# Routed experts: the gate and up biases as pairs of 64-row products, and the next block's transposes ahead of the gated product's second half

## The chip, the cores and the metric

The kernel runs on one core of a Trainium2 chip. The metric is the device time of one execution in microseconds (us), as the median of several runs; lower is better.

## The reference, cut to what matters

Two transformer blocks are computed on 512 tokens of width 1024. The change touches only the last part of the second block, the routed experts (a mixture of 32 experts, 4 per token, in blocks of 128 rows):

```python
def expert_block(args):
    xb, e = args                       # 128 gathered rows, one expert
    gt = jnp.minimum(xb @ w_gate[e] + b_gate[e], SWIGLU_LIMIT)
    up = jnp.clip(xb @ w_up[e] + b_up[e], -SWIGLU_LIMIT, SWIGLU_LIMIT)
    hid = gt * jax.nn.sigmoid(SWIGLU_ALPHA * gt) * (up + 1.0)
    return hid @ w_down[e] + b_down[e]
```

Everything is float32 with 1024 columns; the gate and up biases are one row of 1024 each for every expert.

## The kernel before

The program is a row of stages, each with its own instruction streams for TensorE, VectorE, ScalarE, GpSimd and the DMA queue of SyncE, tied together by semaphores that are written out by hand. Nothing reorders the code: each engine runs its stream in the order in which it is written. A float32 product is split by hand into float32r parts: a high part, rounded by ScalarE (a `Copy` into a float32r tile), and a low part, the difference, made by VectorE. Three products (high by high, high by low, low by high) are added in PSUM.

`stage_mix_route` is the stage ahead of the experts. Beside its own work it loads the expert biases (`bias_gate_up`, 32 rows of gate and up) and splits them into `c.bias`: 32 rows hold the high part, the next 32 the low part, the remaining 64 are zero, and gate and up stand side by side in 2048 columns.

`stage_experts` is the stage of the change. It loops over the blocks of 128 rows (`block_of(it, u)`, two to an iteration; u = 0 is called the even block here, u = 1 the odd one; the profile shows 33 blocks). A block has 12 pieces of weights, each 128 by 2048 numbers. Piece p belongs to chunk q = p // 2: chunks 0 and 2 are the two halves of the gate product, 1 and 3 those of the up product, 4 and 5 the down product into `Y`. For each piece SyncE has loaded the raw weights, ScalarE writes `w_hi` (line 3133), VectorE writes `w_lo` (line 3207), each in a ring of four, and TensorE multiplies (lines 3070 to 3072 for gate and up, 3080 to 3082 for down). ScalarE may overwrite a ring place when the piece four earlier is done.

Around these products stand, on TensorE:

- the bias: at the first piece of each of the chunks 0 to 3 one product of `pick` (128 by 128, with a one in the block's expert rows) with 512 columns of `bias` (line 3067); it opens the accumulation;
- `turn_hidden(j, half)` (line 3044): four transposes of one half of the gated product `hid`, after piece 5 for half 0, and in the middle of piece 9 for half 1. It waits for VectorE (`h_ok`), whose last step of that half is line 3232;
- `turn(b, nth)` (line 3037): eight transposes of the next block's gathered rows into `X`, after piece 9, inside a branch that the last block skips. ScalarE and VectorE then split `X` into `x_hi` and `x_lo` (lines 3137, 3138, 3212, 3213), which the next block's first product waits for.

ScalarE takes the transposed half in `hidden(j, half)` (line 3146) ahead of the next block's first `w_hi`, so that piece stands behind the transposes in its queue; VectorE's `hid_lo` (line 3237), its `pick` (line 3218), its next `w_lo` and `x_lo` stand behind it in turn.

Of the kernel before, what the change touches and what calls it, by code (L numbers as in the profile page):

```python
# [8 lines left out]
F32 = mybir.dt.float32  # L9
F32R = mybir.dt.float32r  # L10
# [3 lines left out]
ACT = mybir.ActivationFunctionType  # L14
ALU = mybir.AluOpType
AX = mybir.AxisListType

P = 128
# [2398 lines left out]
def stage_mix_route(nc, c, a):  # L2417
# [5 lines left out]
    with Stage(nc, "route") as s:  # L2423
# [73 lines left out]
        bd_raw = c.xg[0:3 * EXPERTS, 1, :]  # L2497

# [4 lines left out]
        with s.block() as block:  # L2503

            @block.sync
            def _(sp):
# [12 lines left out]
                for h in range(2):  # L2519
                    sp.dma_start(c.y[EXPERTS * h:EXPERTS * h + EXPERTS, :, :], a["bias_gate_up"]).then_inc(bias_in, 16)  # L2520
# [10 lines left out]
            def _(pool):  # L2531
# [7 lines left out]
                pool.wait_ge(y_low, PAIRED)  # L2539
                pool.memset(c.y[2 * EXPERTS:P, :, :], 0.0).then_inc(cleared, 1)  # L2540
                pool.wait_ge(cleared, 1)
                pool.wait_ge(squared, M)
                pool.memset(c.xg, 0.0).then_inc(cleared, 1)
                pool.wait_ge(cleared, 2)
# [86 lines left out]
            def _(act):  # L2631
# [7 lines left out]
                act.wait_ge(bias_in, 32)  # L2639
                act.wait_ge(cleared, 1)  # L2640
                act.activation(c.bias[:].rearrange("e (g n) -> e g n", g=2), c.y, ACT.Copy).then_inc(bias_high, 1)
# [40 lines left out]
            def _(dve):  # L2682
# [17 lines left out]
                lo_rows = c.bias[lows, :].rearrange("e (g n) -> e g n", g=2)  # L2700
                step(dve.tensor_tensor(lo_rows, c.y[lows, :, :], lo_rows.bitcast(F32), ALU.subtract))
# [109 lines left out]
def stage_experts(nc, c, a, out):  # L2811
# [13 lines left out]
    with Stage(nc, "moe") as s:  # L2825
# [5 lines left out]
        pick = s.sb("pick", [P, P], F32R)  # L2831
        slot, xg, y = c.slot, c.xg, c.y
# [79 lines left out]
        with s.block() as block:  # L2912
# [115 lines left out]
            def _(pe):  # L3028
# [19 lines left out]
                def block_of(it, u):  # L3048
                    j = it * 2 + u
                    with pe.If(j < n):  # L3050
                        pe.wait_ge(x_low, j + 1)
                        pe.wait_ge(picked, j + 1)
                        for p in range(PIECES):
# [8 lines left out]
                            if q < 4:  # L3062

                                out = GU[:, q, :]
                                if not second:
                                    o = D * (q % 2) + CHUNK * (q // 2)
                                    pe.matmul(out, pick[:], bias[:, o:o + CHUNK], start=True, stop=False)
# [5 lines left out]
                            else:  # L3073
                                for f in range(2):
                                    if p == 9 and f == 1:
                                        turn_hidden(j, 1)
# [9 lines left out]
                            if p == 9:  # L3086
                                with pe.If(j + 1 < n):
                                    turn(1 - u, it + u)
# [111 lines left out]
            def _(dve):  # L3200
# [14 lines left out]
                def pick_bias(j):  # L3215

                    e = owner_of(dve, j)
                    dve.tensor_tensor(pick[:], c.ident[:, ds(e, 1)].to_broadcast([P, P]),
                                      c.ident[:, ds(e + EXPERTS, 1)].to_broadcast([P, P]), ALU.add).then_inc(picked, 1)
# [20 lines left out]
                dve.sem_inc(w_low, STARTED)  # L3240
# [270 lines left out]
```

## Time and profile before

| | |
|---|---|
| median of 3 runs | 3331.22 us (3329.69 to 3335.95) |
| span of the profiled execution | 3332.1 us |
| mean granted clock of TensorE | 0.973 of full speed |
| TensorE busy with matmuls | 3127.5 us, 94% |
| VectorE busy | 2668.2 us, 80% |
| ScalarE busy | 1817.5 us, 55% |
| experts' block loop | about 2111 us to 3297 us of the span |

The profiled execution's span is the time from its first to its last instruction, and it is 0.9 us above the median of the runs; there is no separate figure for what lies around it. Busy times are shares of the whole span; the stage of the experts is the last third of it. Matmul durations overlap: one lasts 0.39 us from its start to its modelled end, while the next starts 0.23 us after it, so what a matmul costs is read from start to start.

### The profile page before, as it was taken

What the parts mean: (1) busy time and instruction counts of PE and PEld (TensorE: products, weight loads), DVE (VectorE), ACT (ScalarE), POOL (GpSimd) and SP (SyncE); (2) the same over time, 40 slices, a digit from 0 to 9 for tenths busy, and PEclk for the clock granted to TensorE, in tenths of its full rate; (3) what the DMA queues carried; (4) which work ended last, traced back from release to release, by engine and by line L of the source; (5) the groups of instructions that cost most, each with busy time, mean ns of one, the idle gap of its engine ahead of it and who ended that gap; (6) DMA issues with size and microseconds to landing.
All of it is one profiled execution on the core that took longest, in us unless ns stands there. A gap on an engine that the chain in (4) does not pass through costs nothing. (4 is left out here: it accounts for less than half of the span.)

```text
span 3332.1 us, 47952 instructions
## 1 busy us (share of the span) xinstructions
PE 3127.5 (94%) x16376; PEld 2708.8 (81%) x16376; DVE 2668.2 (80%) x3821; ACT 1817.5 (55%) x2211; POOL 834.3 (25%) x516
## 2 busy tenths in 40 slices
PE   7999788999887999999999888799999999999998
PEld 7996677999887888888888766688888888888885
DVE  6895652995496887878888565899999999999997
ACT  4433442334585333333333344578877777877775
POOL 0000102445321444445545100211211211211212
PEclk9999888999998999999999889899999999999999
DMA  5231031335456998999998414699999999999996
GB/s 142 70 83 39 1 127 64 136 119 175 152 228 250 337 343 320 350 341 331 344 358 318 170 29 165 257 364 356 366 368 354 361 371 363 364 373 367 365 371 252
DMA packets 195750, 853.24 MB, mean 256 GB/s; under 512 B 21776, under 2 KB 104336, under 8 KB 151936
## 3 DMA queue, kind: packets, MB, share of 16 engines
q1 hardware_dynamic: 167712, 700.86, 57.4%
q0 software_dynamic: 27936, 151.02, 11.1%
q8 instruction: 64, 1.05, 0.1%
q14 instruction: 38, 0.31, 0.0%
HBM read 810.39 MB, written 59.24 MB: 261 GB/s over the span
## 5 line engine op out<-in xcount | busy, mean ns | idle before, releaser
L3207 DVE TENSOR_TENSOR moe_w_lo<-all_raw,moe_w_hi 128x2048 fp32r<-128x2048 f32 x298 | 676.2, 2287 | 50.6 <-ACT moe_w_hi L3133 48.2
L3133 ACT ACTIVATE moe_w_hi<-all_raw 128x2048 fp32r<-128x2048 f32 x298 | 569.3, 1916 | 80.0 <-PE moe_GU L3072 60.0
L3072 PE MATMUL moe_GU<-moe_w_hi,moe_x_lo 128*128 128x512 f32 x1056 | 412.3, 390 | 0.0
L3071 PE MATMUL moe_GU<-moe_w_lo,moe_x_hi 128*128 128x512 f32 x1056 | 412.2, 390 | 0.0
L3070 PE MATMUL moe_GU<-moe_w_hi,moe_x_hi 128*128 128x512 f32 x1056 | 411.7, 390 | 0.0
L1889 DVE SCALAR_TENSOR_TENSOR experts_pair<-experts_pair,all_x_first 128x1024 f32<-128x1024 f32 x128 | 156.4, 1222 | 142.6 <-DMA experts_pair<-in_peer_pairs,experts_slot 142.6
L1733 POOL DMA_INDIRECT experts_pair<-in_peer_pairs,experts_slot x128 | 222.4, 1738 | 114.7 <-POOL experts_slot L1730 110.0
L1264 POOL TENSOR_TENSOR score_w_lo<-all_hT,score_w_hi 128x1024 fp32r<-128x1024 f32 x67 | 165.2, 2467 | 303.7 <-DVE all_x_lo L1380 161.4
L1730 POOL COPY experts_slot<-all_pair_id 128x1 uint32 x128 | 152.8, 1194 | 334.1 <-DVE all_h L1901 304.4
L2976 POOL DMA_INDIRECT pair_rows<-all_mixT,all_slot x32 | 48.8, 1526 | 738.2 <-ACT all_mixT L3175 738.2
L3071 PEld LDWEIGHTS moe_GU<-moe_w_lo,moe_x_hi 128*128 128x128 f32 x1056 | 198.6, 188 | 42.1
L3072 PEld LDWEIGHTS moe_GU<-moe_w_hi,moe_x_lo 128*128 128x128 f32 x1056 | 198.6, 188 | 41.7
L3070 PEld LDWEIGHTS moe_GU<-moe_w_hi,moe_x_hi 128*128 128x128 f32 x1056 | 199.0, 188 | 40.6
L3207 DVE TENSOR_TENSOR moe_w_lo<-all_hT,moe_w_hi 128x2048 fp32r<-128x2048 f32 x98 | 222.5, 2284 | 0.1
L3080 PE MATMUL moe_Y<-moe_w_hi,moe_hid_hi 128*128 128x512 f32 x528 | 212.3, 402 | 0.8 <-DVE moe_hid_lo L3237 0.8
L3082 PE MATMUL moe_Y<-moe_w_hi,moe_hid_lo 128*128 128x512 f32 x528 | 206.2, 391 | 0.0
L3081 PE MATMUL moe_Y<-moe_w_lo,moe_hid_hi 128*128 128x512 f32 x528 | 205.8, 390 | 0.0
L3133 ACT ACTIVATE moe_w_hi<-all_hT 128x2048 fp32r<-128x2048 f32 x98 | 187.7, 1915 | 32.5 <-PE moe_GU L3072 18.7
L1749 PE MATMUL experts_H<-all_x_hi,experts_wd_hi 128*128 128x384 f32 x512 | 173.6, 339 | 20.0 <-DVE experts_wd_lo L1871 19.9
L1288 PE MATMUL score_H<-all_x_hi,score_w_hi 128*128 128x384 f32 (+1 forms) x544 | 190.3, 350 | 1.4 <-DVE all_x_lo L1380 1.4
L1290 PE MATMUL score_H<-all_x_hi,score_w_lo 128*128 128x384 f32 (+1 forms) x544 | 189.6, 349 | 0.0
L1289 PE MATMUL score_H<-all_x_lo,score_w_hi 128*128 128x384 f32 (+1 forms) x544 | 189.6, 349 | 0.0
(546 smaller groups left out, 8108.7 us busy)
## 6 DMA issues: line engine op xcount, KB each, us to landing
all_raw<-in_w_moe SPq DMA_DIRECT2D x149, 2048.0 KB, 9.8
all_hT<-in_w_moe SPq DMA_DIRECT2D x49, 2048.0 KB, 9.7
all_hT<-in_peer_wdT SPq DMA_DIRECT2D x128, 512.0 KB, 8.8
all_wu<-in_peer_pairs SPq DMA_DIRECT2D x64, 1024.0 KB, 10.5
peer_gates<-gates_out SPq DMA_DIRECT2D x6, 4096.0 KB, 11.6
experts_gt<-peer_gates SPq DMA_DIRECT2D x32, 768.0 KB, 9.7
all_hT<-in_w_in SPq DMA_DIRECT2D x40, 512.0 KB, 3.8
all_hid<-peer_early SPq DMA_DIRECT2D x60, 192.0 KB, 7.6
```

Of the source, the lines that this page charges most:

```text
L1288: pe.matmul(out, left, c.x_hi[:, k, at:T], start=(k == 0), stop=False)
L1289: pe.matmul(out, left, c.x_lo[:, k, at:T], start=False, stop=False)
L1290: mm = pe.matmul(out, low, c.x_hi[:, k, at:T], start=False, stop=(k == KD - 1))
L1733: pool.indirect_dma_start(out=pair[:, v, :], out_offset=None, in_=a["peer_pairs"][:, :], in_offset=bass.IndirectOffsetOnAxis(ap=slot[:, n: ...
L3070: pe.matmul(out, x_hi[:, kx, :], hi[:, k, :], start=False, stop=False)
L3071: pe.matmul(out, x_hi[:, kx, :], lo[:, k, :], start=False, stop=False)
L3072: mm = pe.matmul(out, x_lo[:, kx, :], hi[:, k, :], start=False, stop=(kx == KD - 1))
L3080: pe.matmul(Y[:, b, :], hid_hi[:, h, :], hi[:, f, cols], start=(h == 0), stop=False)
L3081: pe.matmul(Y[:, b, :], hid_hi[:, h, :], lo[:, f, cols], start=False, stop=False)
L3082: mm = pe.matmul(Y[:, b, :], hid_lo[:, h, :], hi[:, f, cols], start=False, stop=(h == KD - 1))
L3133: act.activation(w_hi[p % RING][:], piece_of(r, p), ACT.Copy).then_inc(w_high, 1)
L3207: dve.tensor_tensor(w_lo[p % RING][:], piece_of(r, p), w_hi[p % RING][:].bitcast(F32), ALU.subtract).then_inc(w_low, 1)
```

## The change

In `stage_experts`, the four bias products of 128 rows by 512 columns per block become four of 64 rows by 512 columns. They are issued as two pairs: at piece 0 the first halves of gate (rows 0 to 63) and up (rows 64 to 127), at piece 4 the second halves. The two of a pair write different PSUM banks. So `bias` now holds gate high, gate low, up high, up low in four groups of 32 rows and 1024 columns, and `pick` has ones in four rows; it is a copy of a column of a new tile `sel`, which VectorE builds with three additions at the start of the stage. Also, the eight transposes of the next block (with their branch) stand in the middle of piece 9, ahead of the wait and the four transposes of the gated product's second half, where they stood after piece 9.

In `stage_mix_route` the biases are loaded by four DMAs instead of two, ScalarE's split is 1024 columns wide instead of 2048, VectorE's low part is two operations of 32 by 1024 instead of one of 32 by 2048, and GpSimd's clearing of rows 64 to 127 is gone.

```diff
@@ stage_mix_route
-                for h in range(2):
-                    sp.dma_start(c.y[EXPERTS * h:EXPERTS * h + EXPERTS, :, :], a["bias_gate_up"]).then_inc(bias_in, 16)
+                for i in range(4):
+                    sp.dma_start(bias_raw[EXPERTS * i:EXPERTS * i + EXPERTS, :], a["bias_gate_up"][:, i // 2, :]).then_inc(bias_in, 16)
...
-                pool.wait_ge(y_low, PAIRED)
-                pool.memset(c.y[2 * EXPERTS:P, :, :], 0.0).then_inc(cleared, 1)
-                pool.wait_ge(cleared, 1)
...
-                act.wait_ge(bias_in, 32)
-                act.wait_ge(cleared, 1)
-                act.activation(c.bias[:].rearrange("e (g n) -> e g n", g=2), c.y, ACT.Copy).then_inc(bias_high, 1)
+                act.wait_ge(bias_in, 64)
+                act.activation(c.bias[:], bias_raw, ACT.Copy).then_inc(bias_high, 1)
...
@@ stage_experts, TensorE
-                                if not second:
-                                    o = D * (q % 2) + CHUNK * (q // 2)
-                                    pe.matmul(out, pick[:], bias[:, o:o + CHUNK], start=True, stop=False)
+                                if not second and q % 2 == 0:
+                                    half = slice(CHUNK * (q // 2), CHUNK * (q // 2) + CHUNK)
+                                    for g in range(2):
+                                        own = slice(2 * EXPERTS * g, 2 * EXPERTS * g + 2 * EXPERTS)
+                                        pe.matmul(GU[:, q + g, :], pick[own, :], bias[own, half], start=True, stop=False)
...
                                     if p == 9 and f == 1:
+                                        with pe.If(j + 1 < n):
+                                            turn(1 - u, it + u)
                                         turn_hidden(j, 1)
...
-                            if p == 9:
-                                with pe.If(j + 1 < n):
-                                    turn(1 - u, it + u)
@@ stage_experts, VectorE
-                    dve.tensor_tensor(pick[:], c.ident[:, ds(e, 1)].to_broadcast([P, P]),
-                                      c.ident[:, ds(e + EXPERTS, 1)].to_broadcast([P, P]), ALU.add).then_inc(picked, 1)
+                    dve.tensor_copy(pick[:], sel[:, ds(e, 1)].to_broadcast([P, P])).then_inc(picked, 1)
...
+                step = chained(dve, chain)
+                step(dve.tensor_tensor(sel[:], c.ident[:, 0:EXPERTS], c.ident[:, EXPERTS:2 * EXPERTS], ALU.add))
+                step(dve.tensor_tensor(sel[:], sel[:], c.ident[:, 2 * EXPERTS:3 * EXPERTS], ALU.add))
+                step(dve.tensor_tensor(sel[:], sel[:], c.ident[:, 3 * EXPERTS:4 * EXPERTS], ALU.add))
                 pick_bias(0)
```

The first place is TensorE at the start of a block. Before, one bias product opens the gate's accumulation (and another stands 25 rows further down, ahead of the up product):

```order
L3061 ISA [waits route_slot_ok,route_ge_high]
L3067 MATMUL moe_GU<-all_bias,moe_pick 128x512 [waits moe_w_low]
L3070 MATMUL moe_GU<-moe_w_hi,moe_x_hi 128x512
L3071 MATMUL moe_GU<-moe_w_lo,moe_x_hi 128x512
L3072 MATMUL moe_GU<-moe_w_hi,moe_x_lo 128x512
```

Now both stand there, and none ahead of the up product (line numbers shift by one):

```order
L3060 ISA [waits route_slot_ok,route_ge_high]
L3068 MATMUL moe_GU<-all_bias,moe_pick 128x512 [waits moe_w_low]
L3068 MATMUL moe_GU<-all_bias,moe_pick 128x512
L3071 MATMUL moe_GU<-moe_w_hi,moe_x_hi 128x512
L3072 MATMUL moe_GU<-moe_w_lo,moe_x_hi 128x512
L3073 MATMUL moe_GU<-moe_w_hi,moe_x_lo 128x512
```

The up bias has moved ahead of 24 products of the gate, and the same holds at piece 4. (The names in brackets are semaphores by number; those of other stages are reused ones.)

The second place is TensorE in piece 9. Before, the gated product's transposes stand between the two halves of the piece, and the next block's after it:

```order
L3082 MATMUL moe_Y<-moe_w_hi,moe_hid_lo 128x512
L3042 REGISTER_ALU
L3044 MATMUL moe_GU<-all_ident,moe_hid 128x128 [waits moe_h_ok]
L3044 MATMUL moe_GU<-all_ident,moe_hid 128x128 x3
L3080 MATMUL moe_Y<-moe_w_hi,moe_hid_hi 128x512
L3081 MATMUL moe_Y<-moe_w_lo,moe_hid_hi 128x512
L3082 MATMUL moe_Y<-moe_w_hi,moe_hid_lo 128x512
...
L3087 COMPARE_AND_BRANCH
L3034 ISA
L3037 MATMUL moe_X<-all_ident,all_mixT 128x128 [waits norm_meaned]
L3037 MATMUL moe_X<-all_ident,all_mixT 128x128 x7
L3087 UNCONDITIONAL_BRANCH
```

Now they come first, with their branch:

```order
L3085 MATMUL moe_Y<-moe_w_hi,moe_hid_lo 128x512
L3077 COMPARE_AND_BRANCH
L3033 ISA
L3036 MATMUL moe_X<-all_ident,all_mixT 128x128 [waits norm_meaned]
L3036 MATMUL moe_X<-all_ident,all_mixT 128x128 x7
L3077 UNCONDITIONAL_BRANCH
L3041 REGISTER_ALU
L3043 MATMUL moe_GU<-all_ident,moe_hid 128x128 [waits moe_h_ok]
L3043 MATMUL moe_GU<-all_ident,moe_hid 128x128 x3
L3083 MATMUL moe_Y<-moe_w_hi,moe_hid_hi 128x512
```

The wait on `h_ok` now stands behind the eight transposes and the end of their branch, and the four transposes of the gated product behind both.

## Rows read from the trace of the kernel before

**Rows 1.** Busy time by engine, 180 us of the experts' loop; a count behind each.
```profile
core 0: us, PE busy (x) PEld busy (x) DVE busy (x) ACT busy (x) POOL busy (x), PEclk, DMA share, GB/s
2300.00:2480.00 180.00, 179.33 (x825) 147.53 (x824) 171.22 (x125) 141.73 (x106) 34.92 (x21) 1.00 0.94 362
```

**Rows 2.** Bias products of before, all: min/median/max ns, first and last start.
```profile
L3067 PE MATMUL moe_GU<-all_bias,moe_pick x132: 389/389/787, 2111.1 to 3278.8; 128*128 128x512 f32 x132
```

**Rows 3.** Timeline of PE, a bias product and the 24 behind it: start, duration.
```profile
2554.82 0.39 PE L3067 MATMUL moe_GU<-all_bias,moe_pick 128*128 128x512 f32 x1
2555.05 0.39 PE L3070 MATMUL moe_GU<-moe_w_hi,moe_x_hi 128*128 128x512 f32 x1
...
2560.26 0.39 PE L3072 MATMUL moe_GU<-moe_w_hi,moe_x_lo 128*128 128x512 f32 x1
```

**Rows 4.** Timeline of PE, attention: 64-row products between others, in five short windows.
```profile
1987.37 0.27 PE L2265 MATMUL attn_X<-all_ident,attn_sc 128*128 128x128 f32 x1
1987.57 0.49 PE L2252 MATMUL attn_S<-all_kT,all_qT 64*128 64x256 f32 x2
1987.89 0.39 PE L2252 MATMUL attn_S<-all_kT,all_qT 64*128 64x256 f32 x2
1988.10 0.39 PE L2252 MATMUL attn_S<-all_kT,all_qT 64*128 64x256 f32 x2
1988.32 0.39 PE L2252 MATMUL attn_S<-all_kT,all_qT 64*128 64x256 f32 x2
1988.64 0.34 PE L2277 MATMUL attn_O<-attn_pT,all_vtok 128*64 128x128 f32 x2
```

**Rows 5.** Timeline of PE in the last block: a product after a wait.
```profile
3292.22 0.49 PE L3080 MATMUL moe_Y<-moe_w_hi,moe_hid_hi 128*128 128x512 f32 x1 [0.83 <-DVE moe_hid_lo L3237]
3292.54 0.39 PE L3081 MATMUL moe_Y<-moe_w_lo,moe_hid_hi 128*128 128x512 f32 x1
```

**Rows 6.** Timeline of PE, piece 9 of an even block.
```profile
2570.50 0.39 PE L3082 MATMUL moe_Y<-moe_w_hi,moe_hid_lo 128*128 128x512 f32 x1
2571.22 0.66 PE L3044 MATMUL moe_GU<-all_ident,moe_hid 128*128 128x128 f32 x4 [0.33 <-DVE moe_hid L3232]
...
2571.96 0.40 PE L3081 MATMUL moe_Y<-moe_w_lo,moe_hid_hi 128*128 128x512 f32 x1
...
2572.89 0.39 PE L3082 MATMUL moe_Y<-moe_w_hi,moe_hid_lo 128*128 128x512 f32 x1
2573.12 1.03 PE L3037 MATMUL moe_X<-all_ident,all_mixT 128*128 128x128 f32 x8
2574.11 0.49 PE L3080 MATMUL moe_Y<-moe_w_hi,moe_hid_hi 128*128 128x512 f32 x1
2574.44 0.39 PE L3081 MATMUL moe_Y<-moe_w_lo,moe_hid_hi 128*128 128x512 f32 x1
```

**Rows 7.** Timeline of PE, piece 9 of the odd block after it.
```profile
2606.70 0.40 PE L3082 MATMUL moe_Y<-moe_w_hi,moe_hid_lo 128*128 128x512 f32 x1
2606.93 0.60 PE L3044 MATMUL moe_GU<-all_ident,moe_hid 128*128 128x128 f32 x4
...
2607.61 0.39 PE L3081 MATMUL moe_Y<-moe_w_lo,moe_hid_hi 128*128 128x512 f32 x1
...
2608.52 0.39 PE L3082 MATMUL moe_Y<-moe_w_hi,moe_hid_lo 128*128 128x512 f32 x1
...
2610.05 0.39 PE L3081 MATMUL moe_Y<-moe_w_lo,moe_hid_hi 128*128 128x512 f32 x1
```

**Rows 8.** Waits from 2120 us on: us in total, times, longest.
```profile
PE moe_GU L3044 <- DVE moe_hid L3232: 5.5, 16, 0.5
```

**Rows 9.** Timelines of ACT, DVE and PE, end of that odd block, next block's start.
```profile
2607.57 0.60 ACT L3146 ACTIVATE moe_hid_hi<-moe_GU 128x512 fp32r<-128x512 f32 x1 [2.43 <-PE moe_GU L3044]
2612.82 0.68 DVE L3213 TENSOR_TENSOR moe_x_lo<-moe_X,moe_x_hi 128x512 fp32r<-128x512 f32 x1
2615.30 0.39 PE L3067 MATMUL moe_GU<-all_bias,moe_pick 128*128 128x512 f32 x1
```

**Rows 10.** Timeline of DVE and ACT, route stage and start of the experts.
```profile
2044.11 1.92 ACT L2641 ACTIVATE all_bias<-all_mixT 128x2048 fp32r<-128x2048 f32 x1 [8.75 <-DMA all_mixT<-in_bias_gate_up]
2094.81 0.23 DVE L2788 TENSOR_SCALAR route_ecmp<-route_end,route_part 128x32 f32<-128x32 f32 x1
2107.30 2.33 DVE L3207 TENSOR_TENSOR moe_w_lo<-all_raw,moe_w_hi 128x2048 fp32r<-128x2048 f32 x1 [0.74 <-ACT moe_w_hi L3133]
```

More of the change, by code:

```diff
@@ L2497, in stage_mix_route @@
         bd_raw = c.xg[0:3 * EXPERTS, 1, :]
+        bias_raw = c.y[:, 0, :]
         ranks, total = acc[:, 0, 0, 0:M * EXPERTS], acc[:, 0, 0, M * EXPERTS:(M + 1) * EXPERTS]
@@ L2538, in _ @@
                 pool.wait_ge(made, 4)
-                pool.wait_ge(y_low, PAIRED)
-                pool.memset(c.y[2 * EXPERTS:P, :, :], 0.0).then_inc(cleared, 1)
-                pool.wait_ge(cleared, 1)
                 pool.wait_ge(squared, M)
                 pool.memset(c.xg, 0.0).then_inc(cleared, 1)
-                pool.wait_ge(cleared, 2)
+                pool.wait_ge(cleared, 1)
                 pool.wait_ge(saved, 16 * M)
@@ L2699, in _ @@
                 lows = slice(EXPERTS, 2 * EXPERTS)
-                lo_rows = c.bias[lows, :].rearrange("e (g n) -> e g n", g=2)
-                step(dve.tensor_tensor(lo_rows, c.y[lows, :, :], lo_rows.bitcast(F32), ALU.subtract))
+                up_lows = slice(3 * EXPERTS, 4 * EXPERTS)
+                dve.tensor_tensor(c.bias[lows, :], bias_raw[lows, :], c.bias[lows, :].bitcast(F32), ALU.subtract)
+                step(dve.tensor_tensor(c.bias[up_lows, :], bias_raw[up_lows, :], c.bias[up_lows, :].bitcast(F32), ALU.subtract))
                 dve.wait_ge(bd_high, 1)
@@ L2831, in stage_experts @@
         pick = s.sb("pick", [P, P], F32R)
+        sel = s.sb("sel", [P, EXPERTS])
         slot, xg, y = c.slot, c.xg, c.y
@@ L3273, in _ @@
                     block_of(it, 0)
-                step = chained(dve, chain)
                 def first_row(m):
@@ L3423, in routed @@
         self.xg, self.y = pairs[:, 0, :, :], pairs[:, 1, :, :]
-        self.bias = self.sb(ctx, "bias", [P, 2 * D], F32R)
+        self.bias = self.sb(ctx, "bias", [P, D], F32R)
         self.geT = self.sb(ctx, "geT", [3 * EXPERTS, M, P], F32R)
```

## The prediction

> **What bounds the kernel now.** I read the page first, then the loop of the experts in 180 us windows, then TensorE's timeline product by product, then the waits of that stretch, and last what the other engines do at a block's end. In the loop TensorE is busy 179.33 of 180 us at full clock (1.00), VectorE 171.22, ScalarE 141.73 [rows 1]. A busy TensorE proves little, since its records overlap, so the pitch counts: from the first to the last of the 24 products behind a bias product it is 5.21 us over 23 steps, 0.2265 us each, and the bias product takes the same step (2554.82 to 2555.05) [rows 3]. Nothing stands between them. So in this loop a product removed from TensorE is 0.2265 us off the end, and one added is as much on it, as long as VectorE keeps up; over this window VectorE has 5% left.
>
> Only two kinds of place leave TensorE's pitch: the transposes, and one wait. The wait is for the gated product (VectorE's line 3232). From 2120 us on, 16 waits of more than noise are put down to it, 5.5 us of PE's idle time [rows 8]. They are one in every second block: the even block shows 0.72 us from the last product to the first transpose [rows 6], the odd one 0.23 [rows 7]. The last of the 16 is in the last block, so 15 lie in blocks that have a next one.
>
> **Part 1, the pairs.** There are 132 bias products [rows 2], four to a block, so 33 blocks and 66 places where a pair will stand. If nothing but the products counted, a pair that runs at once would replace two steps (0.453 us) by one. What it takes to go from 128-row products to 64-row ones and back isn't shown in this loop, but attention shows it at full speed [rows 4]:
> - into the 64-row form: transposes there follow each other at 0.109 us (as the eight of the next block do: 1.03 us less the last one's 0.27, over 7 steps [rows 6]), but the first 64-row products start 0.20 us after the last: 0.09 lost;
> - the weights of the first two can't be loaded ahead: first two to second two 0.32 us, where later ones follow at 0.215 (1987.89 to 1988.32 in two steps): 0.10 lost;
> - out of it: 0.32 us from the last two to the next form, instead of 0.215: 0.10 lost;
> - the first product after it has its own weights exposed: a product that starts cold is followed after 0.32 us instead of 0.2265 [rows 5]: 0.10 lost.
>
> That is 0.39 us of switching to save one step of 0.2265: +0.165 us a place, 66 x 0.165 = **+10.9 us**. The lower bound is a pair that takes one step and nothing else: 66 x 0.2265 = -14.9 us. The upper bound is a pair that doesn't run at once: 66 x 0.39 = +25.7 us. I take the middle value because it is the only one that rows of this case show on both sides of a 64-row stretch.
>
> The Trainium skill (TensorEngine Tiling (Array Packing), Key Properties) says that changing the tiling mode drains TensorE; by that rule, the rows of attention agree, with their 0.09 and 0.10 us. The skill's other page on this (TensorE: Matmul & The Clock Gate, Part 3, Measured speedup vs the span model) gives a pack as one matmul plus some 4 ns for each further tile, with no term for entering or leaving; by it the pairs would save about 14.7 us, and that is my first rival below.
>
> **Part 2, the transposes moved.** I count from the last product before a group of transposes to the second product after it, less two steps. Even block: 2570.50 to 2571.96, less 0.453, is 1.01 us for the four of the gated product with their wait; 2572.89 to 2574.44 is 1.55, less 0.453, 1.10 us for the eight; together 2.11 [rows 6]. Odd block: 0.91 and 1.53 us, less 0.453 each: 0.46 and 1.08, together 1.54 [rows 7]. Afterwards they stand in one run: 0.23 from the product to the first of eight, 7 x 0.109 = 0.76 to the last, then the end of the branch. That end costs something today: the last of the eight starts at 2573.88, the next product at 2574.11, 0.23 later, and is followed after 0.33 [rows 6]. I take 0.23 for it again, then 0.39 for the starts of four transposes with a cold first one (0.66 less 0.27), and 0.35 to the second product: 1.96 less 0.453 = 1.51. So an even block gains 0.60, an odd one 0.03: 15 x 0.60 + 17 x 0.03 = **-9.5 us**. If the branch's end hides under transposes, 0.12 and the 0.06 of the cold start go as well, at most 32 x 0.18 = 5.8 us more. The wait itself must then be over: in the even block the gated product is there at 2571.2, and TensorE would now come to it at 2570.50 + 0.23 + 0.76 + 0.23 = 2571.7, even without the pairs' delay. It has 0.5 us to spare.
>
> **What comes late by it.** The gated product's transposes in an odd block start about 0.76 + 0.23 + 0.33 (the two pairs of that block) = 1.3 us later than now. Behind them in ScalarE's queue are line 3146, the next block's first high part and both halves of `x_hi`; in VectorE's queue `hid_lo`, `pick`, the next low part and `x_lo`. The last of these ends now at 2613.50, the next block starts at 2615.30 [rows 9]: 1.8 us of cover. TensorE itself moves by 0.3, so 0.8 us of cover is left. In an even block the delay is smaller, since the transposes there wait already. ScalarE has 2.43 us idle ahead of line 3146 [rows 9], which takes the delay first. I cost it at nothing; once the cover is gone it costs one for one.
>
> The up bias now comes ahead of the gate's 24 products, which ends the first piece pair 0.39 us later and the second 0.165 later. VectorE's first use of the gate comes far later than the piece's end, and the banks were read before `h_ok` of the block before.
>
> **The rest.** `sel` is three small operations; one of 32 columns takes 0.23 us and VectorE's next step there waits 0.74 us for ScalarE [rows 10], so about 0.1 us shows, once. `pick` as a copy is no longer than before and isn't waited for. In the route stage ScalarE waited 8.75 us for the biases' DMA and then took 1.92 for the split [rows 10]; half as wide it takes about 0.9 less, and four DMAs move the same bytes. Bounds are 1 us either way, and I take 0, since TensorE's products cover that stretch.
>
> **Sum.** +10.9 - 9.5 + 0 = +1.4 us on the profiled execution of 3332.1 us, 3333.5; its span is 0.9 us above the median of the runs, so against that median 3331.2 + 1.4 = **3332.6 us**. No change that can be told: about 0.2% (6.7 us) is what a measurement of this kernel can tell from none.
>
> **Rivals.**
> - *Switching is cheap for float32r* (faster). Attention's products are float32, each two records, and what starts together there may differ from a pair on two row halves. Without any switching cost: -14.9 - 9.5 = -24.4, 3306.8 us; with half of the 0.39 us paid: 66 x (0.195 - 0.2265) = -2.1, with the moves -11.6, 3319.6. For it: these products are twice as long, so loads may hide. Against it: in attention neither load nor drain was hidden. It decides for faster once a place costs under +0.04 us. 25%.
> - *The two of a pair run one after the other* (slower). The two records that start together in attention could be the two of one float32 product. Then a place costs +0.39: +25.7 - 9.5 = +16.2, 3347.4 us. It decides for slower once a place costs over (6.7 + 9.5) / 66 = 0.245 us. 13%.
> - *The wait moves instead of going* (slower). The later transposes use up the 0.8 us of cover and the next block's first product waits for `x_lo`, or VectorE, at 95%, falls behind. If it eats the whole gain: +10.9, 3342 us; 8%.
> - *The change does what its parts cost here* (no change), 54%, with its own range of 3327 to 3338 us.
>
> **How the numbers follow.** The forecast's 54% is almost all of "same"; I put same 0.53, faster 0.26, slower 0.21. The range of 3310 to 3346 us leaves out the pair without any switching (about 11%) and most of the pair in series.
>
> **What the changed profile would show.** (1) The two bias products of a pair start some 10 to 20 ns apart, in the 64-row form. If 0.23 us or more apart, the second rival holds. (2) Last 128-row product to the pair 0.32 us, pair to first product 0.42, that to the second 0.32: in all about 1.07 us from the last product to the second one after the pair, where 0.91 was spent before, one of its four steps further down. If near 0.70, the first rival. (3) PE's waits for line 3232 gone but in the last block, and in both kinds of block 1.96 us from the product before the transposes to the second one after. (4) No wait of TensorE for `x_lo` at a block's start. (5) Block pairs still 71.8 us long or within 0.2 of it. What would make me wrong is (2), since it counts 66 times, and the end of the branch, which counts 32 times.

## The result: 30 us slower, and what the profile after shows

| | before | after |
|---|---|---|
| median of 4 runs beside each other | 3333.59 us (3329.69 to 3336.48) | 3363.59 us (3356.14 to 3367.86) |
| ratio | | 1.0092 (1.0076 to 1.0109) |
| span of the profiled execution | 3332.1 us | 3366.1 us |

The forecast was 3332.6 us, "no change that can be told", with a range of 3310 to 3346. The kernel is slower by 0.9%, outside the range. The page of the changed kernel, first the span, then busy time by engine:

```profile
span 3366.1 us, 47955 instructions
...
PE 3162.9 (94%) x16376; PEld 2694.2 (80%) x16376; DVE 2674.8 (79%) x3825; ACT 1818.3 (54%) x2211; POOL 831.0 (25%) x515
```

The same 180 us of the experts' loop as in [rows 1], columns as there:

```profile
2300.00:2480.00 180.00, 179.57 (x802) 141.31 (x803) 168.01 (x123) 135.91 (x103) 36.30 (x20) 1.00 0.92 352
```

TensorE is as full as before, at the same granted clock (1.00), and gets through 802 matmul records where it got through 825. VectorE and ScalarE do less in the same time, so they aren't the bound: TensorE's own stream has become slower. The page's share of busy time doesn't show it; only the count and the pitch do.

The length of a block is read from TensorE's timeline: the first bias product of the 3rd and of the 33rd block, 30 blocks apart. Before:

```profile
2184.48 0.39 PE L3067 MATMUL moe_GU<-all_bias,moe_pick 128*128 128x512 f32 x1
...
3261.48 0.39 PE L3067 MATMUL moe_GU<-all_bias,moe_pick 128*128 128x512 f32 x1
```

And after:

```profile
2188.88 0.51 PE L3068 MATMUL moe_GU<-all_bias,moe_pick 64*128 64x512 f32 x2
...
3295.20 0.50 PE L3068 MATMUL moe_GU<-all_bias,moe_pick 64*128 64x512 f32 x2
```

(3261.48 - 2184.48) / 30 = 35.90 us a block, and (3295.20 - 2188.88) / 30 = 36.88: 0.98 us more. Over 33 blocks that is 32 us, about the whole loss, so other stages have no part in it that can be told. Two blocks together take 73.8 us, where the prediction had 71.8 within 0.2. This block length repeats better than a single execution's span, because the loop's first bias product starts anywhere between 2104 and 2114 us in the executions profiled here. I use it below beside the medians.

Three places of a block answer to the steps of the prediction. First the pair, TensorE's timeline at a block's start:

```profile
2483.49 0.40 PE L3085 MATMUL moe_Y<-moe_w_hi,moe_hid_lo 128*128 128x512 f32 x1
2483.82 0.51 PE L3068 MATMUL moe_GU<-all_bias,moe_pick 64*128 64x512 f32 x2
2484.25 0.50 PE L3071 MATMUL moe_GU<-moe_w_hi,moe_x_hi 128*128 128x512 f32 x1
2484.59 0.40 PE L3072 MATMUL moe_GU<-moe_w_lo,moe_x_hi 128*128 128x512 f32 x1
```

The two of the pair stand in one row (x2); their single records start 3 to 4 ns apart, where 10 to 20 was forecast. From the last product to the second one behind the pair it is 1.10 us, and 1.07 was forecast.

Second, products with nothing between them, the first and the last of 15 in a row:

```profile
2498.23 0.40 PE L3071 MATMUL moe_GU<-moe_w_hi,moe_x_hi 128*128 128x512 f32 x1
...
2501.49 0.39 PE L3073 MATMUL moe_GU<-moe_w_hi,moe_x_lo 128*128 128x512 f32 x1
```

14 steps in 3.26 us: 0.2324 us each (from the unrounded starts; 0.233 from the rows). In [rows 3] it is 0.2265. The prediction took this pitch as given. Nothing in the diff touches these products.

Third, the moved transposes in piece 9 and the start of piece 10:

```profile
2511.69 0.40 PE L3085 MATMUL moe_Y<-moe_w_hi,moe_hid_lo 128*128 128x512 f32 x1
2511.93 1.04 PE L3036 MATMUL moe_X<-all_ident,all_mixT 128*128 128x128 f32 x8
2512.80 0.60 PE L3043 MATMUL moe_GU<-all_ident,moe_hid 128*128 128x128 f32 x4
2513.15 0.48 PE L3083 MATMUL moe_Y<-moe_w_hi,moe_hid_hi 128*128 128x512 f32 x1
2513.47 0.39 PE L3084 MATMUL moe_Y<-moe_w_lo,moe_hid_hi 128*128 128x512 f32 x1
...
2514.41 0.40 PE L3085 MATMUL moe_Y<-moe_w_hi,moe_hid_lo 128*128 128x512 f32 x1
2514.89 0.49 PE L3083 MATMUL moe_Y<-moe_w_hi,moe_hid_hi 128*128 128x512 f32 x1
```

The transposes are as cheap as hoped, and cheaper: 1.78 us from the product before them to the second behind them, with 1.96 forecast. The four start 0.11 us behind the last of the eight (2511.93 + 7 x 0.109 = 2512.69), so the end of the branch costs nothing. But six products later stands a gap that I hadn't forecast: 0.48 us from 2514.41 to 2514.89, where a step is 0.23. The waits of TensorE from 2120 us on name it, beside the two of the pairs (us in total, times, longest):

```profile
PEld moe_GU L3068 <- issue: 23.9, 65, 0.4
...
PEld moe_Y L3083 <- issue: 16.8, 32, 0.5
...
PEld moe_GU L3071 <- issue: 16.1, 65, 0.2
```

32 times line 3083: once in each block that has a next one, ahead of piece 10. The wait for the gated product of [rows 8] is gone.

### The profile page after: what moved, and what is told of

Same layout as the page of the kernel before. It is cut to its first block and busy times, and to the rows that moved or that the text cites. A ratio compares the mean times of both kernels' runs of the same rounds, so it can differ in the third digit from the quotient of the medians.

```text
span 3366.1 us, 47955 instructions
## 1 busy us (share of the span) xinstructions
PE 3162.9 (94%) x16376; PEld 2694.2 (80%) x16376; DVE 2674.8 (79%) x3825; ACT 1818.3 (54%) x2211; POOL 831.0 (25%) x515
## 5 line engine op out<-in xcount | busy, mean ns | idle before, releaser
L3071 PE MATMUL moe_GU<-moe_w_hi,moe_x_hi 128*128 128x512 f32 x1056 | 427.2, 405 | 0.0
L2975 POOL DMA_INDIRECT pair_rows<-all_mixT,all_slot x32 | 68.2, 2131 | 754.6 <-ACT all_mixT L3175 754.6
L1730 POOL COPY experts_slot<-all_pair_id 128x1 uint32 x128 | 144.2, 1127 | 342.3 <-DVE all_h L1901 312.7
```

What stands on the lines that cost most here:

```text
L3071: pe.matmul(out, x_hi[:, kx, :], hi[:, k, :], start=False, stop=False)
```

## Theories

The loss has three candidates: **addresses** (the slower pitch comes from where the tiles now lie: `bias` is 4096 bytes a partition smaller, and `sel`, 128 bytes a partition, stands behind `pick` and in front of `x_hi`), **pairs** (they cost, and the different form slows the products behind them too), and **moves** (the transposes' new place costs instead of giving). The rival to addresses is that the pitch is a consequence of the pairs or of the new order.

The table has the tiles' addresses, in bytes of a partition modulo 256 (as the program allocates them), with the measured pitch and block length of every kernel. The pitch is that of one even stretch of 14 steps at full clock; the mean of all steps under 0.26 us in the loop is 227.3 to 228.2 ns in the kernels with three equal addresses and 232.4 to 233.1 in those where `x` and `hid` differ from `w`. `x` stands for `x_hi` and `x_lo`, `hid` for `hid_hi` and `hid_lo`, which are the stationary operands of the gate and up products and of the down products; `w` for the eight tiles of `w_hi` and `w_lo`, which are streamed:

| kernel | w | x | hid | pitch gate/up, ns | pitch down, ns | us a block |
|---|---|---|---|---|---|---|
| before | 32 | 32 | 32 | 226.6 | 226.7 | 35.90 |
| after | 32 | 160 | 160 | 232.4 | 232.4 | 36.88 |
| e1_place | 32 | 32 | 32 | 226.6 | 226.6 | 36.24 |
| e2_moves_only | 32 | 32 | 32 | 226.7 | 226.7 | 35.98 |
| e3_pairs_only | 32 | 160 | 160 | 232.4 | 233.3 | 36.72 |
| e4_shift_only | 32 | 160 | 160 | 232.4 | 232.4 | 36.23 |
| e5_shift32 | 32 | 64 | 64 | 233.4 | 233.4 | 36.28 |
| e6_shift_all32 | 64 | 64 | 64 | 226.6 | 226.6 | 35.96 |
| e7_shift_hid | 32 | 32 | 160 | 226.7 | 232.4 | 36.00 |
| e8_moves_swap | 32 | 32 | 32 | 226.6 | 226.6 | 36.14 |
| e9_pairs_placed | 32 | 32 | 32 | 226.7 | 226.6 | 36.25 |
| e10_hid_first | 32 | 32 | 32 | 226.6 | 226.6 | 35.90 |
| e11_shift256 | 32 | 32 (+256) | 32 (+256) | 226.6 | 226.6 | 35.90 |
| e12_sel_first | 160 | 160 | 160 | 226.6 | 226.6 | 36.22 |

## Experiments

### e1_place: the change with the tiles where they lay before

```diff
...
-        self.bias = self.sb(ctx, "bias", [P, D], F32R)
+        self.bias = self.sb(ctx, "bias", [P, 2 * D], F32R)[:, 0:D]
...
-        sel = s.sb("sel", [P, EXPERTS])
...
         warm = s.sb("warm", [P, 1])
+        sel = s.sb("sel", [P, EXPERTS])
```

`bias` takes its old 8192 bytes a partition again and uses half, and `sel` is the last tile of the stage instead of standing behind `pick`.

> The changed kernel with every tile of the experts' stage at the SBUF address that it has in the kernel before: the bias tile keeps its 8 KB a row (half unused) and the new tile sel is allocated last. The instructions are the same. In the changed kernel the pitch of the 128x512 products is 0.2325 us throughout the experts' loop, against 0.2268 in the kernel before. Theory P (placement: the moved tiles slow the streams): the pitch falls back to about 0.227 and the time by about 33 x 0.8 = 25 us, to some 3338 us. Theory M (the 64-row products leave TensorE in a slower rhythm, which it keeps): the pitch stays at 0.2325 and the time at 3360 to 3366 us. Theory D (the pitch depends on what VectorE, ScalarE and the DMAs do meanwhile): no change either, unless addresses are what they collide on.

3340.5 us (8 runs) against 3328.47 for the kernel before on the same chip (23 runs), ratio 1.004 (1.0026 to 1.0055). The products in a row, first and last of 15 again:

```profile
2492.37 0.39 PE L3071 MATMUL moe_GU<-moe_w_hi,moe_x_hi 128*128 128x512 f32 x1
...
2495.54 0.39 PE L3073 MATMUL moe_GU<-moe_w_hi,moe_x_lo 128*128 128x512 f32 x1
```

3.17 us for 14 steps: the pitch of before is back, with the pairs and the new order in place. A block is 36.24 us, 0.64 less than in the changed kernel: 33 x 0.64 = 21 us are the tiles' place; by the medians it is 18 of the 30 (+30.0 against +12.0). The mean of all steps from product to product in the loop says nearly the same: 232.7 ns after, 227.7 here, 5.0 ns over 134 steps a block, 0.66 us, of which piece 10's wait gives 0.06 back (0.48 us after, 0.54 here).

### e2_moves_only: only the transposes moved

```diff
                                     if p == 9 and f == 1:
+                                        with pe.If(j + 1 < n):
+                                            turn(1 - u, it + u)
                                         turn_hidden(j, 1)
...
-                            if p == 9:
-                                with pe.If(j + 1 < n):
-                                    turn(1 - u, it + u)
```

> The kernel before with the moved transposes alone: bias products of 128 rows in their old places, tiles where they were. Read from the changed kernel: the transposes cost 1.33 us a block there, against 2.11 and 1.54 us in even and odd blocks, so 15 x 0.78 + 17 x 0.21 = 15 us gained; the wait of the down product's piece 10 for hid_lo, which is new, costs 0.35 us a block, 11 us. Theory M or P: pitch 0.227, so the sum is -4 us, ratio 0.999. If the pitch is 0.2325 here too, the order of the transposes is what sets it, and the time is some 20 us above the kernel before.

3332.56 us (10 runs) against 3328.47, ratio 1.0016 (1.0005 to 1.0027); a block 35.98 against 35.90. The forecast for this part alone was -9.5 us, and -4 us was expected of this run. That had a new wait at piece 10 in it, 0.35 us a block as read from the changed kernel; in even blocks here it is longer. TensorE's waits from 2120 us on:

```profile
PEld moe_Y L3082 <- DVE moe_w_lo L3206: 15.2, 16, 1.2
...
PEld moe_Y L3082 <- issue: 8.8, 17, 0.5
...
PE moe_Y L3082 <- DVE moe_hid_lo L3236: 8.4, 16, 0.8
```

The 16 waits of [rows 8] are now 16 waits of piece 10 for `hid_lo`, and longer. TensorE in an even block:

```profile
2567.39 1.03 PE L3037 MATMUL moe_X<-all_ident,all_mixT 128*128 128x128 f32 x8
2568.26 0.60 PE L3044 MATMUL moe_GU<-all_ident,moe_hid 128*128 128x128 f32 x4
...
2569.86 0.40 PE L3084 MATMUL moe_Y<-moe_w_hi,moe_hid_lo 128*128 128x512 f32 x1
2570.76 0.49 PE L3082 MATMUL moe_Y<-moe_w_hi,moe_hid_hi 128*128 128x512 f32 x1 [0.50 <-DVE moe_hid_lo L3236]
```

And VectorE in the same block:

```profile
2567.14 0.69 DVE L3231 SCALAR_TENSOR_TENSOR moe_hid<-moe_up,moe_ga 128x512 f32<-128x512 f32 x1
2567.75 2.28 DVE L3206 TENSOR_TENSOR moe_w_lo<-all_raw,moe_w_hi 128x2048 fp32r<-128x2048 f32 x1
2569.95 0.68 DVE L3236 TENSOR_TENSOR moe_hid_lo<-moe_GU,moe_hid_hi 128x512 fp32r<-128x512 f32 x1
```

VectorE runs without a gap from the gated product to `hid_lo` (ends 2570.63), and piece 10 starts 0.13 us behind it. No order of TensorE's transposes makes that earlier. In the kernel before, the same three operations of VectorE stand at 2570.48, 2571.09 and 2573.29:

```profile
2573.29 0.68 DVE L3237 TENSOR_TENSOR moe_hid_lo<-moe_GU,moe_hid_hi 128x512 fp32r<-128x512 f32 x1
```

It ends at 2573.97, and the product behind the eight transposes starts at 2574.11 [rows 6], 0.14 us later. So that product, the first of piece 10, was already waiting for `hid_lo`. The 0.23 us between the last transpose and it, which I took for the end of the branch, was this wait. Over the loop piece 10 starts 0.13 to 0.14 us behind the end of `hid_lo` in every block of the kernel before, even and odd.

Summed over TensorE's stream by place (mean over blocks, from the starts, with the step to piece 10 counted against a plain one of 0.227): ahead of and inside the transposes an even block gains 0.68 us and an odd one 0.09, a little more than the 0.60 and 0.03 forecast; at piece 10 an even block loses 0.68 and an odd one 0.27.

### e8_moves_swap: the same, with hid_lo ahead of the last low part

```diff
                         unit(j, 1)
-                        low(it, u, 11)
                         hidden(j, 1)
+                        low(it, u, 11)
```

> The moves alone as in e2_moves_only, with VectorE's hid_lo of the second half ahead of its last low part (w_lo of piece 11) instead of behind it. In e2_moves_only the first product of piece 10 starts 0.49 us (odd blocks) and 0.90 us (even blocks) after the product ahead of it, because it waits for hid_lo, which stands behind 2.2 us of w_lo on VectorE. Theory H (that queue is the wait): the gap falls to 0.23 to 0.3, the moves give 0.78 us in an even block and 0.2 in an odd one, and the kernel is 10 to 15 us faster than before, ratio 0.996. Rival: VectorE now idles about 1 us for ScalarE's hid_hi in every block, has no slack for it (34.0 us of work in 35.9), and w_lo is late for TensorE: same as or slower than before.

3337.99 us (10 runs) against 3329.5 (13 runs), ratio 1.0027 (1.0013 to 1.004); a block 36.14. Slower than e2. The waits of VectorE and TensorE:

```profile
DVE moe_hid_lo L3236 <- ACT moe_hid_hi L3145: 65.2, 33, 2.3
...
PEld moe_Y L3082 <- issue: 17.1, 33, 0.5
...
PEld moe_GU L3067 <- issue: 16.1, 32, 0.5
```

VectorE now stands idle 2.0 us a block for ScalarE's `hid_hi`, which needs the transposes, and is then late for the next block: its first product starts 0.13 us behind the end of `x_lo` (line 3067 waits 32 times). Piece 10 still waits in every block (17.1 us). That shows the second limit. From the first of the four transposes to piece 10 it is 2.09 us here, 2.10 in an odd block of e2, and 2.09 in the changed kernel (2512.80 to 2514.89 above): transposes, 0.60 us of ScalarE, 0.69 of VectorE. The transposes themselves and the six products behind them fill only 1.83 us of it. In the kernel before, the eight transposes of the next block stood in that gap and covered it.

### e10_hid_first: the gated product's transposes first, the next block's right behind

```diff
                                         turn_hidden(j, 1)
+                                        with pe.If(j + 1 < n):
+                                            turn(1 - u, it + u)
...
-                            if p == 9:
-                                with pe.If(j + 1 < n):
-                                    turn(1 - u, it + u)
```

> The kernel before with the two groups of transposes side by side as well, but in the other order: the gated product's four first, the next block's eight right behind them, then the six products of piece 9. hid_hi and hid_lo start as early as before, and piece 10 comes no earlier. Theory H (the chain gated product, transposes, ScalarE, VectorE's hid_lo, piece 10 sets what this spot can give): an odd block gains the 0.2 us of the switches and of the branch, an even block 0 to 0.1, since hid_lo ends 0.14 us ahead of piece 10 there; 3 to 5 us in all, ratio 0.999. Rival (the spot is worth 0.2 and 0.78 us as read from the transposes alone): 10 us or more.

3329.7 us (12 runs) against 3329.51 (20 runs), ratio 1.0008 (0.9997 to 1.0019); a block 35.90, as before. The expected 3 to 5 us didn't come either. TensorE in an odd block:

```profile
2531.27 1.04 PE L3037 MATMUL moe_X<-all_ident,all_mixT 128*128 128x128 f32 x8
2532.06 0.48 PE L3082 MATMUL moe_Y<-moe_w_hi,moe_hid_hi 128*128 128x512 f32 x1
...
2533.31 0.40 PE L3084 MATMUL moe_Y<-moe_w_hi,moe_hid_lo 128*128 128x512 f32 x1
2533.64 0.49 PE L3082 MATMUL moe_Y<-moe_w_hi,moe_hid_hi 128*128 128x512 f32 x1
```

The last of the eight transposes starts at 2531.27 + 7 x 0.109 = 2532.03, and the product behind them, with the branch's end between, 0.03 us later. It has nothing to wait for at this place, and the step is that of 28 ns which follows the gated product's four transposes in the kernel before, where no branch ends. So the branch's end costs nothing. The time won is lost again at piece 10 (0.33 us from 2533.31 to 2533.64), which starts 0.13 to 0.14 us behind the end of `hid_lo` in every block, as before. Those 0.14 us, which the expectation took for slack, are the distance at which it always starts when it has waited. The cover is kept and the transposes stand in one run, but even blocks still wait for the gated product and both kinds then for VectorE. TensorE's order in this spot isn't what limits it.

### e3_pairs_only and e9_pairs_placed: only the pairs, at the change's addresses and at those of before

e3 is the changed kernel with the transposes put back:

```diff
                                     if p == 9 and f == 1:
-                                        with pe.If(j + 1 < n):
-                                            turn(1 - u, it + u)
                                         turn_hidden(j, 1)
...
+                            if p == 9:
+                                with pe.If(j + 1 < n):
+                                    turn(1 - u, it + u)
```

> The changed kernel with the transposes back in their old places: the pairs alone, tiles placed as in the changed kernel. The pairs cost 1.09 us from the last product to the second after them, as forecast, which is 0.18 us a place and 12 us in all. Theory M or P: the pitch stays at 0.2325, which adds about 25 us, so 37 us above the kernel before, about 3370 us. If the order of the transposes sets the pitch, it is 0.227 and the kernel 12 us above, about 3345 us.

3358.8 us (4 runs) against 3328.47, ratio 1.0093 (1.0069 to 1.0117): all of the loss by the medians without the moves, and still two causes in one. A block is 36.72 us, so by that measure the moves cost the changed kernel 0.16 us a block (36.88). I had expected 37 us, as a sum of two separate costs; 27 is what 33 x 0.82 gives, because TensorE no longer waits for the gated product (0.24 us to its first transpose in even blocks, where it was 0.73). e9 is e3 with the edit of e1:

```diff
...
-        self.bias = self.sb(ctx, "bias", [P, D], F32R)
+        self.bias = self.sb(ctx, "bias", [P, 2 * D], F32R)[:, 0:D]
...
-        sel = s.sb("sel", [P, EXPERTS])
...
         warm = s.sb("warm", [P, 1])
+        sel = s.sb("sel", [P, EXPERTS])
```

> The pairs alone, transposes in their old places, every tile of the stage at the address of the kernel before. The price of the pairs free of the pitch. My forecast's sum gave 0.165 us a place, 66 places, 10.9 us; the pairs of the changed kernel, read at their place, take 1.09 us to the second product behind them, 0.18 us a place. Theory (placement and the pairs add up): pitch 0.227 us, loop 35.9 + 0.36 = 36.25 us a block, 12 us slower than before, ratio 1.0036. Rival (pairs disturb the streams behind them whatever the addresses): pitch above 0.230 and 36.6 us a block.

3344.13 us (5 runs) against 3329.51, ratio 1.004 (1.0025 to 1.0055); a block 36.25, 0.35 over before: 33 x 0.35 = 11.6 us, with 10.9 forecast; by the medians it is 14.6. TensorE's timeline around a pair:

```profile
2486.14 0.39 PE L3073 MATMUL moe_GU<-moe_w_hi,moe_x_lo 128*128 128x512 f32 x1
2486.46 0.50 PE L3068 MATMUL moe_GU<-all_bias,moe_pick 64*128 64x512 f32 x2
2486.89 0.50 PE L3071 MATMUL moe_GU<-moe_w_hi,moe_x_hi 128*128 128x512 f32 x1
2487.23 0.40 PE L3072 MATMUL moe_GU<-moe_w_lo,moe_x_hi 128*128 128x512 f32 x1
```

0.32, 0.43 and 0.34 us where four steps of 0.2266 stood: +0.18 a place. Summed over all steps of a block, the pairs cost 0.41 us, 0.20 a place, because a few products behind each pair are slow too. The step to the gated product's first transpose falls by 0.11 in the mean of both kinds of block, since TensorE comes to that wait later, the transposes and piece 10 give back 0.05 of that, and 0.35 is left.

Comparing e9 with e1, where only the moves differ, gives 36.25 against 36.24: with the pairs in place and the tiles where they lay the moves are worth nothing either way.

### e4_shift_only: the kernel before with an unused tile of 128 bytes

```diff
         pick = s.sb("pick", [P, P], F32R)
+        sel = s.sb("sel", [P, EXPERTS])
```

> The kernel before with one unused tile of 128 bytes a row allocated behind pick: x_hi, x_lo and the tiles after them lie 128 bytes further, as they do modulo 2048 in the changed kernel. No instruction changes. Theory P with the 128 bytes as the cause: pitch 0.2325, time about 3358 us. Theory M, or P with the 4096 bytes as the cause: pitch 0.227 and no change.

3342.08 us (10 runs) against 3328.47, ratio 1.0042 (1.0029 to 1.0054); 3358 was expected. A tile that nothing reads or writes makes the kernel 14 us slower. First and last of 15 products:

```profile
2489.16 0.39 PE L3071 MATMUL moe_GU<-moe_w_hi,moe_x_hi 128*128 128x512 f32 x1
...
2492.41 0.40 PE L3073 MATMUL moe_GU<-moe_w_hi,moe_x_lo 128*128 128x512 f32 x1
```

The pitch is 232.4 ns, as in the changed kernel. A block grows by only 0.33 us and not by 0.64, because the slower stream no longer has to wait for VectorE: in even blocks the step from the last product to the gated product's first transpose falls from 0.73 us to 0.23. And in its odd blocks the product behind the eight transposes starts 0.03 us after the last of them, with the branch where it was: the branch's end costs nothing when `hid_lo` is ready.

### e5, e6, e7 and e11: which address counts

e5 puts 32 bytes in the same place, e6 puts 32 bytes ahead of `w_hi` (which shifts everything), e7 puts 128 bytes between `hid` and `hid_hi`, and e11 puts 256 bytes behind `pick`. All start from the kernel before; each is a single run, read by its pitch and not by its time.

The edit of e5, and of e11 with 64 in place of 8:

```diff
         pick = s.sb("pick", [P, P], F32R)
+        gap = s.sb("gap", [P, 8])
```

> The kernel before with one unused tile of 32 bytes a row behind pick: x_hi, x_lo and all tiles after them lie 32 bytes further, the weights w_hi and w_lo where they were. Both addresses are 32 modulo 512 in the kernel before (pitch 0.227 us); the shift by 128 bytes made them 32 and 160 (pitch 0.2324). Theory R (relation: the stationary operand's address against the moving one's, modulo 512 or so): 32 and 64 differ, so the pitch is 0.230 or more, and the loop 36.2 us a block. Theory A (some absolute alignment of the tiles behind pick, of which 32 is a good one and 160 a bad one): the pitch may be either; 0.227 would refute R at this distance.

> The kernel before with 256 unused bytes a row behind pick: x_hi, x_lo and hid_hi, hid_lo at 288 modulo 512, the weights at 32. Theory R with a period of 512 bytes or more: the pitch is off 0.227 (0.230 or more). With a period of 256, 0.227.

That of e6:

```diff
+        gap = s.sb("gap", [P, 8])
         w_hi = [s.sb(f"w_hi{i}", [P, PIECE], F32R) for i in range(RING)]
```

> The kernel before with the unused 32 bytes ahead of w_hi: the weights and everything after them lie 32 bytes further, both at 64 modulo 512 (0 modulo 64). Theory R: the relation is kept, so the pitch stays at 0.227 us and the loop at 35.9 us a block. Theory A: the pitch is that of e5_shift32, since x_hi and x_lo are at the same address in both; or, if an alignment to 64 bytes is what a read of the moving operand wants, it falls below 0.227.

And of e7:

```diff
         hid = s.sb("hid", [P, CHUNK])
+        gap = s.sb("gap", [P, 32])
```

> The kernel before with 128 unused bytes a row ahead of hid_hi alone: only the stationary operands of the down product (pieces 8 to 11) and the small tiles after them move; x_hi, x_lo, ga, up, sg and hid stay. If the address of TensorE's stationary operand is what counts, the down product's pitch rises to 0.232 and the gate and up products' stays at 0.227, so a block is 48 x 0.0055 = 0.26 us longer. If it is what VectorE or ScalarE read or write (ga, up, sg, hid), nothing changes.

e5: 3339.77 us, pitch 233.4. e6: 3334.55 us, pitch 226.6. e7: 3337.43 us. e11: 3329.02 us, pitch 226.6. (Before beside them: 3329.5.) e7 tells the most, because one kernel holds both pitches. Its gate products, with `x` unshifted, and its down products, with `hid_hi` shifted by 128 bytes:

```profile
2484.61 0.39 PE L3071 MATMUL moe_GU<-moe_w_hi,moe_x_hi 128*128 128x512 f32 x1
...
2487.78 0.39 PE L3073 MATMUL moe_GU<-moe_w_hi,moe_x_lo 128*128 128x512 f32 x1
...
2494.88 0.39 PE L3081 MATMUL moe_Y<-moe_w_hi,moe_hid_hi 128*128 128x512 f32 x1
...
2498.13 0.40 PE L3083 MATMUL moe_Y<-moe_w_hi,moe_hid_lo 128*128 128x512 f32 x1
```

14 steps in 3.17 us and 14 in 3.25. So it is a product's own operands that decide, not the stage's memory traffic as a whole. A block grows by 0.10 us of the 0.26 expected: the waits for the gated product and at piece 10 shrink by 0.12 in the mean of both kinds of block. A shift of the stationary operand alone by 32 or 128 bytes is slow; by 256 it is not; and a shift of both by the same 32 bytes is not. (In e6 the first ten or so steps of a block are mostly 228 to 236 ns before they settle at 226.6, and the block is 0.06 us longer than before. Why isn't known.)

### e12_sel_first: the changed kernel, with sel ahead of w_hi

```diff
+        sel = s.sb("sel", [P, EXPERTS])
         w_hi = [s.sb(f"w_hi{i}", [P, PIECE], F32R) for i in range(RING)]
...
         pick = s.sb("pick", [P, P], F32R)
-        sel = s.sb("sel", [P, EXPERTS])
```

> The changed kernel with sel allocated ahead of w_hi instead of behind pick: the weights lie 128 bytes further, so that w_hi, w_lo, x_hi, x_lo, hid_hi and hid_lo are all at 160 modulo 512. Theory R: pitch 0.227 us, a block 36.24 us, time that of e1_place, about 3340 us. Theory A (x_hi's own address is bad at 160): pitch 0.2325 and 3360 us.

3342.52 us (6 runs) against 3329.51, ratio 1.0037 (1.0022 to 1.0052); a block 36.22.

```profile
2488.03 0.39 PE L3071 MATMUL moe_GU<-moe_w_hi,moe_x_hi 128*128 128x512 f32 x1
...
2491.21 0.39 PE L3073 MATMUL moe_GU<-moe_w_hi,moe_x_lo 128*128 128x512 f32 x1
```

Every tile of the table is at 160 modulo 256, where in the changed kernel only the stationary ones were, and the pitch is 226.6. One line moved, no work changed, and 22 us are back by the block's length (33 x 0.66), 17 by the medians (+30.0 against +13.0). With e1 (36.24 us a block) it is the best form of the whole change found, and still slower than the kernel before. Nothing tried here is faster than that one by more than the noise.

## Why the prediction was wrong, point by point

- **What bounds the kernel now.** The bound was read rightly (TensorE's stream, nothing between products), but the pitch of 0.2265 us was carried over as a constant of the product's shape. It depends on the tiles' addresses, and the change moves them. There was no term for it in the sum and no rival for it. This is the step that failed by most: 0.64 us a block, 21 us, with the pairs and the moves in place (e1 against the changed kernel), and 0.33 us on the kernel before (e4). The kernel's diff did show a new tile behind `pick` and a smaller one in front.
- **Part 1, the pairs: right, with some luck in the sum.** +10.9 us forecast, +11.6 measured (e9). The pairs themselves cost more, 0.41 us a block or 13.6 us, for the slow products further behind had no term; 0.06 a block comes back because TensorE then waits less for VectorE. The three gaps are as forecast, with 0.32, 0.43, 0.34 us for 0.32, 0.42, 0.32. The rivals "switching is cheap" and "one after the other" both fall: the two start 3 to 4 ns apart, and the place still costs. The Trainium skill (TensorE: Matmul & The Clock Gate, Part 3, Measured speedup vs the span model) gives a pack as one matmul plus some 4 ns for each further tile: by that rule, the 3 to 4 ns between the two starts agree. The gaps at entering and leaving the form are what made this pack a loss.
- **Part 2, the transposes moved: wrong, -9.5 us forecast (-0.29 a block), -0.01 to +0.16 us a block measured** (-0.01: e1 against e9; +0.08: e2 against before; +0.16: the changed kernel against e3). The gains at the transposes came (0.68 and 0.09 us for 0.60 and 0.03). The reading "that end costs something today", 0.23 us for the branch, failed: it was piece 10's wait for `hid_lo`, and the branch's end costs nothing (e10).
- **What comes late by it: wrong.** "I cost it at nothing" rested on the cover of `x_lo` at the next block's start, and that did hold: no wait for `x_lo` showed. But the first consumer of what stands in those queues isn't the next block's first product, it is piece 10, six products on, and it had no slack. I had listed `hid_lo` in VectorE's queue and not asked who takes it first.
- **The rival "the wait moves instead of going"** (8%) had the right outcome for the moves, +10.9 us in all, but by another wait than the one named.
- **The rest** (`sel`, `pick`, the route stage) was tested by no run alone. e1 and e9 both carry it, and their medians, 12.0 and 14.6 us above before, leave few us for it beside the pairs' 11.6.

Sum by the runs, one added after the other (before, e9, e1, after): pairs 0.35, moves -0.01, addresses 0.64, together 0.98 us a block, the 36.88 less 35.90 measured; times 33 it is 32 us, with 30.0 in the medians. In another order the shares differ. Each added alone to the kernel before, they cost 0.35 (e9), 0.08 (e2) and 0.33 (e4), 0.76 together. Most of what is missing is the wait for the gated product, 0.50 us in each even block of the kernel before: the pairs alone or the slower stream alone are in part paid out of it (0.13 us are left of it in e9, none in e4), and it can be used up only once.

What stays open is why the addresses matter. The runs show the relation (modulo 256 bytes, between the two operands of one product, at the distances 0, 32, 128 and 256), not the mechanism, and no other distance or shape was tried.

## What to carry to other kernels

When a change adds, drops or resizes a tile in on-chip memory, compare the addresses of all tiles behind it, and compare the pitch of untouched products in the two traces before explaining anything else; allocate small new tiles last. Costs measured one at a time don't add up while an engine still has a wait that each of them can shorten. When a step is moved earlier on an engine, ask what it was covering where it stood, and follow each delayed result to its first consumer. A pair of half-height products doesn't pay when it must be entered and left for a single step saved; here that costs 0.18 us a place at the pair itself, and 0.20 with the products behind it.

## What the runs showed of the hardware that I had not expected

Products of 128x128 by 128x512 in float32r, back to back at full clock, follow each other at 226.6 ns when the stationary and the streamed operand start at equal addresses modulo 256 bytes of a partition, and at 232.4 to 233.4 ns when they are 32 or 128 bytes apart: 2.6 to 3% of the whole stream. With unequal addresses the steps also become uneven, 228 to 241 ns in a pattern that repeats every seven gate and up products in the changed kernel (228, 230, 233, 241, 232, 231, 232), while at equal ones most are 226 or 227 (86 in 100 in e11, 69 in e6) and the others, nearly all within the first ten or so behind a gap in e1 and e11, up to 240.

The Trainium skill (TensorE: Matmul & The Clock Gate, Part 2, Step-by-step: what each phase is for) says that TensorE reads the streamed operand and the weights through two independent ports, so that loading the next weights takes nothing from the running matmul. Taken by itself, that gives the operands' addresses no part in the pitch. The pitch of e4 against before differs by 5.8 ns with nothing but an unused tile between them, so here the measurement decides. What makes it so, no run shows.
